# Both RWKV head groups as one chain of 16 chunk matrices, with the triangular inverse held as 32-row blocks

## The reference, cut to what matters

```python
def token_mixer(h, w_in, ...):
    p = h @ w_in
    p_r, p_m, p_g = jnp.split(p, [RWKV_COLS, RWKV_COLS + MLSTM_COLS], axis=-1)
    y_r = rwkv7_branch(p_r, ...) @ branch_w_rwkv
    y_m = mlstm_branch(p_m, ...) @ branch_w_mlstm
    g_r, g_m = jnp.split(jax.nn.sigmoid(p_g), 2, axis=-1)
    return (g_r * y_r + g_m * y_m) @ w_out

def step(s, inp):                       # inside rwkv7_branch, one token
    r_t, w_t, k_t, v_t, a_t, b_t = inp
    sa = jnp.einsum('bhvk,bhk->bhv', s, a_t)
    s = s * w_t[:, :, None, :] + sa[..., None] * b_t[:, :, None, :] + v_t[..., None] * k_t[:, :, None, :]
    return s, jnp.einsum('bhvk,bhk->bhv', s, r_t)
```

## Time and profile before

| quantity | value |
|---|---|
| median of 3 runs | 1440.77 us (1438.9 to 1441.27) |
| span of the profiled execution | 1437.0 us |
| PE busy | 1419.4 us, 99% of the span |
| DVE busy | 1048.7 us, 73% |
| ACT busy | 298.9 us, 21% |
| POOL busy | 72.2 us, 5% |
| part of the chain that ended last that is PE | 97% |

### The profile page before, as it was taken

The page is one execution under the profiler, slowest core; times in us unless marked ns, Lnnn a source line. Parts: engine busy times, 40 slices in busy tenths (PEclk is TensorE's granted clock), DMA queues, the critical chain, the costliest instruction groups (busy, mean ns, idle before and its releaser), DMA issues.

```text
span 1437.0 us, 29272 instructions
## 1 busy us (share of the span) xinstructions
PE 1419.4 (99%) x12848; PEld 1332.5 (93%) x12848; DVE 1048.7 (73%) x1792; ACT 298.9 (21%) x586; POOL 72.2 (5%) x142
## 2 busy tenths in 40 slices
PE   7999999999999999999999999999999999999998
PEld 3999999898988999999999999988898889999998
DVE  5899888787634669987988886787972456756656
ACT  3111102532223031110031110045222311211101
POOL 7100000000000000000000000000000000000000
PEclk9999999999999999999999999999999999999999
DMA  9998876243422657887758876364432247466440
GB/s 348 336 335 302 306 290 195 89 132 104 117 62 90 227 188 260 296 300 292 248 193 266 285 275 235 127 166 132 133 103 61 61 147 263 148 206 205 179 145 30
DMA packets 214046, 283.03 MB, mean 197 GB/s; under 512 B 13288, under 2 KB 177504, under 8 KB 213920
## 3 DMA queue, kind: packets, MB, share of 16 engines
q1 hardware_dynamic: 194976, 211.11, 45.0%
q0 software_dynamic: 17952, 69.21, 13.2%
q10 hardware_dynamic: 992, 0.85, 0.2%
HBM read 280.10 MB, written 1.05 MB: 196 GB/s over the span
## 4 chain that ended last, share of the span: by engine, by line
PE 97%; DMA 1%; SPq 1%; DVE 1%; issue 0%; ACT 0%; ACTq 0%; DVEq 0%
PE ps L1792 96%; DMA arena<-in_ada_w_dram 1%; PE ps L1796 1%; SPq L549 0%; SPq L544 0%; DVE arena L1651 0%; DVE hT L1777 0%; DVE arena L1646 0%; DVE x L1191 0%; ACT xn L680 0%; ACTq L254 0%; SPq L542 0%; SPq L541 0%; DVEq L1776 0%; ACTq L994 0%
## 5 line engine op out<-in xcount | busy, mean ns | idle before, releaser
L1792 PE MATMUL ps<-hT,ring 128*128 128x128 f32 (+2 forms) x2448 | 399.4, 319 | 1.3 <-ACT hT L680 1.3
L1792 PEld LDWEIGHTS ps<-hT,ring 128*128 128x128 f32 (+1 forms) x2448 | 348.1, 190 | 35.5 <-issue 8.6
L1792 PE MATMUL ps<-y_both,arena 128*128 128x128 f32 x2304 | 266.6, 275 | 1.0 <-issue 1.0
L1792 PEld LDWEIGHTS ps<-y_both,arena 128*128 128x128 f32 x2304 | 261.8, 192 | 1.5 <-issue 1.5
L1792 PEld LDWEIGHTS ps<-arena 64*64 64x64 f32 (+1 forms) x3792 | 221.4, 153 | 17.0 <-issue 11.2
L1792 PE MATMUL ps<-arena 64*64 64x64 f32 (+3 forms) x3792 | 235.4, 243 | 1.3
L1792 PE MATMUL ps<-arena,ring 128*128 128x128 f32 (+1 forms) x1312 | 186.5, 294 | 0.0
L1792 PEld LDWEIGHTS ps<-arena,ring 128*128 128x128 f32 x1312 | 171.3, 192 | 6.6
L1018 DVE SCALAR_TENSOR_TENSOR ada_acc<-ada_stage,cond,ada_acc 128x1024 f32<-128x1024 f32 (+1 forms) x119 | 149.0, 1252 | 5.8 <-DMA ada_stage<-in_ada_w_dram 2.2
L1792 PE MATMUL ps<-y_both,ring 128*128 128x128 f32 (+1 forms) x1024 | 150.8, 301 | 0.0
L1792 PEld LDWEIGHTS ps<-y_both,ring 128*128 128x128 f32 x1024 | 138.6, 192 | 6.4
(11 more groups left out here) (306 smaller groups left out, 1371.8 us busy)
## 6 DMA issues: line engine op xcount, KB each, us to landing
ring<-in_ffn_w_in_dram SPq DMA_DIRECT2D x86, 1024.0 KB, 7.8
ada_stage<-in_ada_w_dram POOLq DMA_DIRECT2D x66, 1024.0 KB, 5.9
ring<-in_ffn_w_out_dram SPq DMA_DIRECT2D x44, 1024.0 KB, 6.2
ring<-in_mix_w_in_dram SPq DMA_DIRECT2D x46, 512.0 KB, 5.0
ring<-in_mix_w_in_dram SPq DMA_DIRECT2D x12, 1024.0 KB, 5.7
ring<-in_mix_w_in_dram SPq DMA_DIRECT2D x6, 1536.0 KB, 6.2
ring<-in_mix_w_out_dram SPq DMA_DIRECT2D x8, 1024.0 KB, 5.2
arena<-in_ada_w_dram SPq DMA_DIRECT2D x6, 1024.0 KB, 13.7
```

Of the source, the lines that this page charges most:

```text
L1792: return nc.tensor.matmul(out_, lhsT, rhs, start=start, stop=stop, **kw)
```

## The change

Both groups go through one chain. All 16 values of `i` (4 head pairs x 2 token tiles x 2 heads, each with two chunks) are handled in one batch, and a batch has one PSUM bank instead of two half banks.

The inverse is held in 32-row blocks. `n16`, `o32`, `xt`, `p2`, `p2t` are tiles of 16 x 32 columns: partition quarter r holds the 32x32 diagonal block r of the two chunks. The steps `p2`, `p4`, `p8`, `xt 2`, `xt 4`, `xt 8`, `g32`, `xt 32` are then each 16 x 4 matmuls of 32x32 on the four diagonal 32x32 tiles of the array. The last merging step is two batches of 32 such matmuls (`g64`, and `xo`, the off-diagonal block of the inverse), and ACT and DVE put the full 64x64 inverse together in `xf`, whose zero block POOL fills. `uz` then uses `xf`.

The masks become smaller, and N is computed by 32x32 outputs (`n`, `o64`), the other three products as `mrb` (64x64) and `mk` (64x128, a half each in two places).

The 96 gate steps stand in 12 places instead of 24, with up to 7 steps in one; 26 of them come at the end. The transposes of y all stand between branch products 1 and 2 of m. SP's wait before the third branch weight is for `qt` instead of `qt 1`.

```diff
-GATE_PLACES = (("num", 4), ("heads", 4), ("masks 0 a", 8), ("masks 0 b", 4), ("inverse 0 p", 2), ("inverse 0 a", 2), ("inverse 0 b", 2),
-               ("inverse 0 c", 2), ("uz 0", 2), ("y 0 a", 5), ("y 0 b", 4), ("y 0 c", 2), ("next", 3),
...
-               ("inverse 1 c", 4), ("uz 1", 2), ("y 1 a", 5), ("y 1 b", 4), ("y 1 c", 2), ("tail", 14))
+GATE_PLACES = (("num", 6), ("a", 5), ("b", 6), ("c", 6), ("d", 7), ("e", 7), ("f", 7), ("g", 7), ("h", 7),
+               ("i", 7), ("j", 5), ("tail", 26))
...
-        m_t = carve(8, 4, 64)
-        m_n = carve(3, 8, 64)
-        p2, p2t, p4t, xt = (carve(8, 64) for n in range(4))
+        xf = carve(16, 64)
...
+        n16, nt16, o32, xt, p2, p2t = (carve(16, 32) for n in range(6))
...
+                dv.wait_ge(*PE.at(l, "n"))
+                masked(n16, "n16", 0)
+                dv.wait_ge(*DV.last(l))
+                flipped("nt16", nt16, n16)
...
+                for r in range(4):
+                    rows, at = slice(32 * r, 32 * r + 32), 32 * (r % 2)
+                    free(V.tensor_copy(xf[rows, :, at:at + 32], xt[rows, :, :]))
...
+                quarter = [slice(32 * r, 32 * r + 32) for r in range(4)]
...
+                def blocks(label, bank, lhsT, rhs):
+
+                    for i in range(16):
+                        for rows in quarter:
+                            last = mm(ps[rows, bank, 32 * i:32 * i + 32], lhsT[rows, i, :], rhs[rows, i, :])
+                    last.then_inc(*PE.step(label))
...
+                for q, t, h, hh in heads:
+                    ar, bt, kt, hats = sets[q // 2]
+                    at = 32 * (2 * q + t)
+                    for r, rows in enumerate(quarter):
+                        last = mm(ps[rows, h, at:at + 32], ar[hh, q % 2, t, 0, rows],
+                                  bt[hh, q % 2, t * P + 32 * r:t * P + 32 * r + 32])
+                last.then_inc(*PE.step("n"))
...
+                pe.wait_ge(*DV.at(l, "nt16"))
+                pe.wait_ge(*AC.at(l, "o64"))
+                blocks("p2", 2, nt16, n16)
+                gates("a")
+                turned("v", 0, 3)
+                pe.wait_ge(*AC.at(l, "p2"))
+                pe.wait_ge(*DV.at(l, "xt 1"))
+                pe.wait_ge(*DV.at(l, "o32"))
+                blocks("xt 2", 0, p2, xt)
+                pe.wait_ge(*DV.at(l, "p2t"))
+                blocks("p4", 1, p2t, p2)
```

More of the change, by code:

```diff
@@ L920, in _ @@
                 gates("num")
-                gates("heads")
-                for g in range(2):
[L924 to L965, removed]
@@ new lines, in _ @@
+                last.then_inc(*PE.step("n"))
+                pe.wait_ge(*DV.at(l, "gates 1"))
+                for q, t, h, hh in heads:
+                    ar, bt, kt, hats = sets[q // 2]
+                    at = 32 * (2 * q + t)
+                    for c in range(2):
+                        last = mm(ps[quarter[2 * c + 1], 2 + h, at:at + 32], ar[hh, q % 2, t, 0, quarter[2 * c + 1]],
+                                  bt[hh, q % 2, t * P + 64 * c:t * P + 64 * c + 32])
+                last.then_inc(*PE.step("o64"))
@@ new lines, in _ @@
+                pe.wait_ge(*DV.at(l, "xt 8"))
+                blocks("g32", 1, o32, xt)
+                pe.wait_ge(*DV.at(l, "kr 1"))
+                for q, t, h, hh in heads:
+                    i = 4 * q + 2 * t + h
+                    for c in chunks:
+                        last = mm(ps[c, 4 + i // 8, 64 * (i % 8):64 * (i % 8) + 64], mk[c, i, 0:64], v_tm[c, q, t, hh])
+                last.then_inc(*PE.step("z0"))
+                pe.wait_ge(*DV.at(l, "x32"))
+                pe.wait_ge(*AC.at(l, "g32"))
@@ new lines, in _ @@
+                blocks("xt 32", 0, p2t, p2)
+                gates("e")
+                pe.wait_ge(*AC.at(l, "turned b 1"))
+                turned("k", 1, 2)
+                pe.wait_ge(*DV.at(l, "xt 32"))
+                for i in range(16):
+                    for c in range(2):
+                        last = mm(ps[quarter[2 * c], 1, 32 * i:32 * i + 32], o64[quarter[2 * c + 1], i, :],
+                                  xt[quarter[2 * c + 1], i, :])
+                last.then_inc(*PE.step("g64"))
@@ new lines, in _ @@
+                gates("f")
+                pe.wait_ge(*DV.at(l, "x64"))
+                pe.wait_ge(*AC.at(l, "g64"))
+                for i in range(16):
+                    for c in range(2):
+                        last = mm(ps[quarter[2 * c], 0, 32 * i:32 * i + 32], p2t[quarter[2 * c], i, :],
+                                  p2[quarter[2 * c], i, :])
+                last.then_inc(*PE.step("xo"))
+                gates("g")
+                pe.wait_ge(*PO.at(None, f"xf {l}"))
+                pe.wait_ge(*DV.at(l, "xf"))
@@ new lines, in _, with chunks_of @@
+                pe.wait_ge(*AC.at(l, "xo"))
+                for n, bank in enumerate((3, 1, 2, 0)):
+                    for i in range(4 * n, 4 * n + 4):
+                        for c in chunks:
+                            last = mm(ps[c, bank, i % 4 * P:i % 4 * P + P], xf[c, i, :], az[c, i, :])
+                    last.then_inc(*PE.step(f"uz {n}"))
+                gates("h")
+                pe.wait_ge(*AC.at(l, "uz 2"))
+                pe.wait_ge(*DV.at(l, "uz 3"))
+                def chunks_of(t, first, end):
+                    for c in range(max(2 * t, first), min(2 * t + 2, end)):
+                        yield c, chunks[c % 2]
@@ L2429, in _ @@
+                gates("j")
+                pe.wait_ge(*DV.at(l, "chain 2"))
+                for q, t, h, hh in heads:
+                    for c, cc in chunks_of(t, 1, 4):
+                        last = mm(y_of(q, t, h)[cc, :], qt[hh, 2 * q + t, cc], state(q, c)[hh, :],
+                                  start=False, stop=True, skip_group_check=True)
+                last.then_inc(*PE.step("y"))
                 pe.wait_ge(*AC.at(l, "low g"))
-                pe.wait_ge(*DV.at(l, "chain 1 2"))
```

504 lines of the change are left out of this document (259 added, 245 removed), and 1 row of the table GATE_PLACES.

## The result

The changed kernel takes 1454.05 us (median of four runs, 1449.67 to 1454.31) against 1441.02 for the kernel before on the same chip: a ratio of 1.0087, 95% interval 1.0071 to 1.0103. The forecast of 1415 was wrong, and so was its sign: the kernel became 0.9% slower. The time is above the range, 1407 to 1435. The profiled run took 1449.67 us, of which the span is 1447.9. It is the fastest of the four: the other three lie together at 1453.8 to 1454.3 us, with a mean granted clock of 0.985 to 0.988 instead of 0.989, so the profiled spans differ by 10.9 us where the medians differ by 13.0.

A forecast was written before the change was run, and what follows sets the result against it. PE's own list of work was taken to bound the kernel. Savings 6.4 + 1.6 + 0.2 + 2.3 + 3.4 less 0.9 and 0.3 gave 12.7 us a layer, 25.4 in both: 1415 us, range 1407 to 1435.

The forecast's parts named there:

- PE's instructions arrive too late: Rival: dense batches of 128 records wait for instruction packets; 1436 us, or 1425 if half wait; chance 0.09.
- (a): Eight inverse steps as 32x32 records on four diagonal tiles, at 8.3 ns a record: saves 6.4 us a layer.
- (b): Last merging step, g64 and xo as 64 records each at 16.6 ns: saves 1.6 us a layer.
- (c): Mask products n, o64, mrb, mk take 4.29 us instead of 4.46: saves 0.2 us a layer.
- (d): Stalls between dependent inverse steps are covered by gate lumps or other batches: all 2.3 us a layer go.
- (e): Small runs between gate steps fall from 21 to 11, at 0.34 us each: saves 3.4 us a layer.
- (h): At the end, DVE's making of all y_r, 5.5 us, is covered by branch products: costs nothing.
- (f): Six changes of tile shape within PE's runs, charged 0.15 us each: adds 0.9 us a layer.
- (g): New wait at the chain's head, p2 for n16 masked and transposed on DVE: adds 0.3 us a layer, bounds 0 to 0.8.

The follow-up runs named there:

- spread: Changed kernel with the tail's 26 gate steps cut to 11 and places a, b, c raised to 12 each: 1459.55 us, ratio 1.0140.
- late5: Changed kernel with SP fetching the weights of gate column 5 only once batch p8 is done: 1448.65 us, ratio 1.0065.
- both probes: Kernel before with 512 unread matmuls ahead of m_t of group 0 in each layer, of 32x32 or of 64x64: 1501.39 and 1500.69 us.
- fine_late: Kernel `fine` with the weights of gate column 5 fetched only once batch p4 is done: 1427.46 us, ratio 0.9921.
- fine: Changed kernel with gate steps laid in 20 lumps and the tail, also inside p4, p8 and xt 32: 1432.65 us, ratio 0.9942.
- thin: Changed kernel with each of the eight inverse steps cut to 8 of its 16 matrices, so output differs: 1414.58 us.
- probe32: Kernel before with 512 unread 32x32 matmuls on four diagonal tiles ahead of m_t of group 0 in each layer: 1501.39 us.

## Why the prediction was wrong

**The step that failed** is the rival "PE's instructions arrive too late". The prediction had the mechanism, the count of 254 instructions to a packet and the nine dense batches, and gave it 0.09 and a time of 1425 to 1436. Three things in it were wrong.

- Its size. It took 1.14 us, a packet's transfer as q8's share in the earlier trace rows gives it, for the time between packets. The transfer does take 0.9 to 1.4 us, but from packet to packet it is mostly 3.4 to 3.8 where PE waits, and 3.33 at the least in any run. So 256 small instructions need some 3.5 us, 27 ns a record, and a batch at 8.3 ns can win nothing unless slower work stands in the same packet. The rows of before could not show this: their runs of small records cost 29.1 ns each on the diagonal, and what is denser is short (`m_n` with 32 records, and a run of 96 in 1.84 us from 403.52 on) with gate steps on both sides. I took "no gaps in before" for "packets are fetched ahead enough".
- Its argument against. "A gate lump of 10 records follows most batches" is true, but four places have two batches and more in a row (`n`, `o64`, `mrb`, `p2`; `xt 2`, `p4`; `xt 4`, `p8`; `g32`, `z0`, `xt 32`), and there all six gaps of layer 0 stand. `spread` shows that larger lumps elsewhere don't help.
- What follows from it. Among the gaps and tiny matmuls the clock stood at 1.2 GHz for 17 us of layer 0, which cost about 7 us, and no term held that. The bulk transfers ahead of a packet doubled two gaps (`late5`).

**Point by point.**

- (a) and (b) held: 8.3 ns a record for 32x32 in fours. `g64` and `xo` were forecast at 16.6 ns; the row below, `g64`, gives (429.78 - 428.65 - 0.15) / 64 = 15.3, and `xo` (433.00 to 434.13) the same.

```profile
428.65 1.20 PE L1817 MATMUL ps<-arena 32*32 32x32 f32 x64
429.78 3.29 PE L1817 MATMUL ps<-hT,ring 128*128 128x256 f32 x14
```

- Of the rules of the Trainium skill: the page "TensorEngine Tiling (Array Packing)", Restrictions and Gotchas, says that different row tiles cannot use one PSUM bank at once, and the page "TensorE: Matmul & The Clock Gate", section "Wait — 56ns, not 53.3ns?", gives about 25 ns as the least time from start to start. The trace disagrees with both here: four row tiles write one bank at 8.3 ns a record. Yet a train of nothing but small matmuls came out at 29 ns a record in both probes, for another reason than that page's.
- (c), (d), (e) and (h) held as a sum: `fine_late` has the prices and almost no gaps. Its layer 1 should take 87.1, 9 x 0.34 = 3.1 for nine more small runs, and 1.7 of idle time: 91.9. It takes 92.00. Layer 0: 87.1 + 3.1 + 4.5 = 94.7, and it takes 95.27. No wait for DVE or ACT stands in layer 0 of after.
- (f) held. In `fine`, a run of `z0` and half of `xt 32` takes 429.78 - 427.08 = 2.70 us, and 0.15 + 64 x 0.0291 + 64 x 0.0083 is 2.54; 0.16 is left for the change of shape, where 0.15 was charged.

```profile
427.08 2.76 PE L1826 MATMUL ps<-arena 64*64 64x64 f32 x128
429.78 2.43 PE L1826 MATMUL ps<-hT,ring 128*128 128x256 f32 x10
```

- (g) seems to fail and doesn't. Layer 1 of after has a stall of 1.70 us ahead of `p2`, and the profile puts it down to DVE:

```profile
1083.48 1.26 PE L1817 MATMUL ps<-arena 32*32 32x32 f32 x127 [1.70 <-DVE arena L1671]
1086.92 0.18 PE L1817 MATMUL ps<-arena 32*32 32x32 f32 x1 [2.18 <-issue]
```

But `p2` needs only DVE's transpose `nt16`, which ended at 1081.71, and ACT's copy `o64`, which ended at 1081.33, and the next gap comes 127 records later. So this too is a packet's end: its packet started at 1080.9, behind a bulk transfer, and PE went on 2.6 us later. With it, layer 1 has 10.1 + 1.7 = 11.8 us of gaps; 87.1 + 11.8 and some 3.7 of half clock (an estimate row by row, as for layer 0) are 102.6, against 103.26.

With the clock at 2.4 GHz and most gaps gone, the change was worth 4.6 and 7.9 us in the two layers of `fine_late`, like for like, not 12.7: the price of the cover that the packets need is nine more small runs and what idle time is left. That the change's own 11 lumps and tail would win the 12.7 without gaps rests on layer 1 of `thin` and is worked out, not measured, since no run had the packets arrive sooner.

What stays open: why it is 3.5 us from one packet to the next and why a packet waits for a bulk transfer in progress, and what exactly brings the clock down. Nor do the runs say whether a transfer on another queue would delay a packet in the same way.

## What to carry to other kernels

Before making matmuls smaller, count PE's instructions: in this kernel float32 matmuls cost four each, and in stretches with nothing larger, 256 of them took about 3.5 us, 3.3 at the least. Lay large matmuls into every such stretch, into the middle of a batch if need be, and keep bulk transfers out of the densest ones. Gaps with no reason at equal distances in instructions are the mark of it; count the records between them before believing a named releaser.

## What the runs showed of the hardware

- PE's instruction packets start mostly 3.4 to 3.8 us apart where PE waits for them (3.33 at the least, in `probe32`), for a transfer of 0.9 to 1.4 us. Every idle stretch of PE of over 0.7 us in the mixers, in all ten runs other than before, ends 2.2 to 2.9 us behind the start of a packet.
- A packet that falls due during a bulk transfer of 1 MB starts as that ends: gaps of 4.4 and 4.6 us, and 2.2 and 2.3 with the transfer moved.
- Four 32x32 tiles on the diagonal overlap in one PSUM bank: 8.3 ns a record.
- At the same rate of instructions and with gaps of 1.6 to 1.8 us, TensorE was granted 1.2 GHz in a train of 32x32 matmuls (it fell just behind a first gap of 3.90 us) and 2.4 in one of 64x64 (first gap 2.87 us). At 1.2 GHz a gate record took up to 0.42 us instead of 0.218.
